# Five gate tiles of a hybrid decoder step move from behind the recurrence into the turns of its heads

## The chip, the core and the metric

The kernel runs on one core of a Trainium2 chip, as one launch. The metric is the time of one execution in microseconds (us) of the device. Five engines take part: TensorE (PE in the profile), VectorE (DVE), ScalarE (ACT), GpSimd (POOL) and SyncE (SP), which only issues transfers. Each engine works through its own list of instructions in order and waits at semaphores for the others.

## The reference

One layer of a decoder with two groups of mixers, for 256 tokens of a prompt and 8 sequences of 8 new tokens, so 320 token columns in all. What matters here is the input projection and the second group, a gated linear recurrence over eight heads of 128 channels:

```python
h = rms_norm(x, norm1[l])
z = h @ w_in[l]
u, q, f, i, g = jnp.split(z, [...])            # pooling input, then 8 heads each of q, f, i, g
...
forget = lb + (1.0 - lb) * jax.nn.sigmoid(f)
logf, k_in, q_f = jnp.log(forget), 1.0 - forget, jax.nn.silu(q)
o, S_new = hgrn2_recurrence(heads(q_f), heads(k_in), heads(i), heads(logf), S_prev[l])
o = o * lax.rsqrt(jnp.mean(o * o, axis=-1, keepdims=True) + EPS)   # per head
o = o * hg_norm[l]
o = o.reshape(B, T, HG_WIDTH) * jax.nn.silu(g)                     # the output gate
mix = jnp.concatenate([pool_out, o], axis=-1) @ w_o[l]
x = x + mix
```

A SwiGLU feed-forward of width 5632 and a last norm follow. All is in fp32.

## The kernel before

**Tiles.** Every projection is cut into tiles of 128 output channels, called units here, with running numbers: 8 of the pooling group, then `H0` on three for each head (forget, query, value), then from `G0` on eight gate tiles (one for each head), then 16 of the output projection from `O0` on, then the feed-forward. A unit of `w_in` is 16 tiles of 128x128 weights; for each, TensorE makes three matmuls over the 320 token columns (weights high x activations high, high x low, low x high), so 48 matmuls. `unit` runs eight weight tiles, then what is given as `between[0]`, the other eight, then `between[1]`. Units alternate between two PSUM banks `zb[0]` and `zb[1]`.

**Splits.** The weights of a unit are loaded by SP into `raw` (two buffers, 1 MB each; a load waits until the unit two before it is split), and split into a high part by ScalarE (`split_hi`, L682) and a low part by VectorE (`split_lo`, L1013), two pieces each. A high piece waits until TensorE has used the same piece of the unit two before. The low piece waits for the high piece. VectorE reads a finished unit from PSUM (`scaled`, L1022), and a unit waits until the unit two before it has been read.

**The recurrence.** It runs in turns of three units. While TensorE works on the forget, query and value units of head h, the recurrence of head r = h - 1 is woven in, in this order (L572): half of the forget unit, `rec_scores(r)`, the other half, `rec_state(r)`, half of the query unit, `rec_out(r)`, the other half, `rec_stat(r)` (the mean of squares over the channels of a head, L391), the value unit, `rec_bcast(r)` (L397 to L400: the reciprocal root of each token is spread over all partitions; it waits for `odiag`, the diagonal matrices that `rec_rms` makes on VectorE).

```python
unit(n, par_, a_rhs, between=(at(rec_scores) if r is not None else extra[0], at(rec_state)))
unit(n + 1, 1 - par_, a_rhs, between=(at(rec_out), at(rec_stat)))
unit(n + 2, par_, a_rhs, between=(extra[1], at(rec_bcast) if not last else None))
```

In the same turn VectorE does, in order (L1289): split of unit n+1, placing of the scores (`rec_scores`), `rec_sample_lo`, reading of the forget unit into `zf`, `rec_state`, split of n+2, `rec_sample_state`, `products(h)` (the products of forget factors, L1177), reading of the query unit into `zq`, split of n+3, `rec_rms(r)` (a reciprocal, four small Newton steps, two diagonals: L1255, L1082 to L1092), `queries(h)` (L1184, L1190), reading of the value unit, `rec_norm(r)`, `rec_lo(r)`. ScalarE does: split of n+1, `rec_tokens`, `forget(h)` (sigmoid of `zf`, then the factors `t`, on which `products` waits), split of n+2, `rec_squares(r)`, the transfers of states, `sigmoid_q(h)`, split of n+3, `rec_std(r)` (the square root, L825; it ends in `ostd`, on which `rec_rms` waits), `rec_hi(r)`. GpSimd makes keys (L1490, L1498) and queries (L1504) of head h, and the decayed sample states.

Heads 0 and 7 are handled at the ends; heads 1 to 6 as r lie in a loop of three rounds with two turns each.

**The gate tiles.** The last turn has the recurrence of head 7 and the units of gates 0, 1 and 2; the units of gates 3 to 7 stand alone behind it, with the `rec_bcast` of head 7 after five weight tiles of gate 3 (L588). A gate costs: VectorE reads the unit into `zf`; ScalarE takes its sigmoid (L839); GpSimd multiplies (L1537); VectorE sums the two parts of the head's mixed output into `go` (L1281), multiplies by the gate (L1285); ScalarE and VectorE split the result again (L843, L1025). The output projection takes the mixed output of head h as its weight tile 8 + h.

Of the kernel before, what the change touches and what calls it, by code (L numbers as in the profile page):

```python
# [26 lines left out]
P = 128  # L27
D = 2048
KD = D // P
# [7 lines left out]
PW = 1024  # L37
# [4 lines left out]
HEADS = 8  # L42
# [21 lines left out]
G0 = H0 + 3 * HEADS  # L64
O0 = G0 + HEADS
# [27 lines left out]
def hybrid_kernel(nc, x_prompt, x_sample, cache_pool, state_hgrn, lb_param, norm1, w_in, w_pool, pool_scale,  # L93
# [12 lines left out]
    with ctx:  # L106
# [73 lines left out]
        go = vv  # L180
# [111 lines left out]
        def _(sp):  # L292
# [27 lines left out]
            with sp.Fori(0, HEADS // 2) as i:  # L320
                for k in range(2):
                    for j, part in enumerate((2, 1, 3)):
                        load(H0 + 6 * i + 3 * k + j, (3 * k + j) % 2, win_v, (0, KD),
                             part * PW + (2 * i + k) * P)
            with sp.Fori(0, HEADS // 2) as i:
                for k in range(2):
                    load(G0 + 2 * i + k, k, win_v, (0, KD), 4 * PW + (2 * i + k) * P)
# [22 lines left out]
        def _(pe):  # L350
# [141 lines left out]
            def rec_scores(r):  # L492
# [32 lines left out]
                pe.wait_ge(unit_read, H0 + 3 * r + 3)  # L525
# [46 lines left out]
            def window(n, par_, r, extra=(None, None), last=False):  # L572

                def at(f):
                    return (lambda: f(r)) if r is not None else None
                unit(n, par_, a_rhs, between=(at(rec_scores) if r is not None else extra[0], at(rec_state)))
                unit(n + 1, 1 - par_, a_rhs, between=(at(rec_out), at(rec_stat)))
                unit(n + 2, par_, a_rhs, between=(extra[1], at(rec_bcast) if not last else None))

            window(H0, 0, None, (lambda: pool_states(NG - 1), lambda: pool_product(NG - 1)))  # L580
            window(H0 + 3, 1, 0)
            with pe.Fori(0, (HEADS - 2) // 2) as i:
                window(H0 + 6 + 6 * i, 0, 2 * i + 1)
                window(H0 + 9 + 6 * i, 1, 2 * i + 2)

            window(G0, 0, HEADS - 1, last=True)

            def last_bcast(k):  # L588
                if k == 4:
                    rec_bcast(HEADS - 1)  # L590
            unit(G0 + 3, 1, a_rhs, after_tile=last_bcast)
            with pe.Fori(0, (HEADS - 4) // 2) as i:
                for k in range(2):
                    unit(G0 + 4 + 2 * i + k, k, a_rhs)
# [77 lines left out]
        def _(act):  # L672
# [96 lines left out]
            def forget(h):  # L769

                act.wait_ge(unit_read, H0 + 3 * h + 1)
                after(act, q_ready, h)
                act.activation(sgm[:, :], zf[:, :], ACT.Sigmoid).then_inc(zf_sig, 1)
# [6 lines left out]
            def sigmoid_q(h):  # L780
                act.wait_ge(unit_read, H0 + 3 * h + 2)
# [50 lines left out]
            def gate(h):  # L832

                gate_sigmoid(h)
                gate_split(h)

            def gate_sigmoid(h):
                act.wait_ge(unit_read, G0 + h + 1)
                act.activation(sgm[:, :], zf[:, :], ACT.Sigmoid).then_inc(g_sig, 1)  # L839
# [5 lines left out]
            def window(n, par_, h, r):  # L845
# [3 lines left out]
                forget(h) if h is not None else gate(0)  # L849
                split_hi(n + 2, par_)  # L850
                rec_squares(r)
                if h is not None:
                    load_s0(r + 1)
                rec_stores(r)
                sigmoid_q(h) if h is not None else gate(1)
                split_hi(n + 3, 1 - par_)
                rec_std(r)
                if h is None:
                    gate(2)
                else:  # L860
                    rec_hi(r)


# [7 lines left out]
            forget(0)  # L871
            split_hi(H0 + 2, 0)
            sigmoid_q(0)
# [5 lines left out]
            with act.Fori(0, (HEADS - 2) // 2) as i:  # L879
                window(H0 + 6 + 6 * i, 0, 2 * i + 2, 2 * i + 1)  # L880
                window(H0 + 9 + 6 * i, 1, 2 * i + 3, 2 * i + 2)

            act.wait_ge(out_done, 32)
            window(G0, 0, None, HEADS - 1)
            split_hi(G0 + 4, 0)
            gate_sigmoid(3)
            rec_hi(HEADS - 1)
            gate_split(3)
            with act.Fori(0, (HEADS - 4) // 2) as i:
                for k in range(2):  # L890
                    split_hi(G0 + 5 + 2 * i + k, 1 - k)
                    gate(4 + 2 * i + k)
# [103 lines left out]
        def _(dve):  # L996
# [274 lines left out]
            def gate(n, par_, h):  # L1271

                gate_read(n, par_)
                gate_apply(h)

# [3 lines left out]
            def gate_apply(h):  # L1279
# [3 lines left out]
                dve.wait_ge(osum, h + 1)  # L1283
                dve.wait_ge(g_act, h + 1)
# [3 lines left out]

            def window(n, par_, h, r):  # L1289

                split_lo(n + 1, 1 - par_)
                if r is not None:
                    rec_scores(r)
                    rec_sample_lo(r)
                scaled(n, par_, zf[:, :]).then_inc(unit_read, 1)
                if r is not None:
                    rec_state(r)
                if h is None:
                    gate_apply(0)
                split_lo(n + 2, par_)  # L1300
                if r is not None:
                    rec_sample_state(r)
                else:
                    pool_means(NG - 1)
                    dve.wait_ge(t_ones, 1)
                if h is not None:
                    products(h)
                    scaled(n + 1, 1 - par_, zq[:, :]).then_inc(unit_read, 1)
                else:
                    gate(n + 1, 1 - par_, 1)  # L1310
                split_lo(n + 3, 1 - par_)
                if r is not None:
                    rec_rms(r)
                if h is not None:
                    queries(h)
                if h is not None:
                    if r is None:
                        pool_lo(NG - 1)
                        dve.wait_ge(sc_zero, 1)
                    done(n + 2)  # L1320
                    out, src = thrice(v_rep, zb[par_])
                    dve.tensor_tensor(out, src, thrice(v_rep, rbc)[1], MUL).then_inc(v_thrice, 1)
                    scaled(n + 2, par_, vv[:, :]).then_inc(unit_read, 1)
                else:
                    gate(n + 2, par_, 2)
                if h is not None and r is not None:
                    rec_norm(r)
                    rec_lo(r)

            window(H0, 0, 0, None)  # L1330
            window(H0 + 3, 1, 1, 0)
            with dve.Fori(0, (HEADS - 2) // 2) as i:
                window(H0 + 6 + 6 * i, 0, 2 * i + 2, 2 * i + 1)
                window(H0 + 9 + 6 * i, 1, 2 * i + 3, 2 * i + 2)

            window(G0, 0, None, HEADS - 1)
            split_lo(G0 + 4, 0)
            gate_read(G0 + 3, 1)
            rec_norm(HEADS - 1)
            rec_lo(HEADS - 1)  # L1340
            gate_apply(3)
            with dve.Fori(0, (HEADS - 4) // 2) as i:
# [248 lines left out]
```

## Time and profile before

| | |
|---|---|
| median of 3 runs | 1489.78 us (1488.51 to 1493.13) |
| the profiled execution | 1493.66 us |
| span of its instructions | 1491.4 us |
| mean granted TensorE clock | 0.992 of full speed |
| busy: PE, DVE, ACT, POOL | 1460.7, 804.9, 550.8, 188.2 us |
| stages | pooling units to 99 us; heads to 395 us, gates alone to 428 us, output projection to 541 us, feed-forward to 1477 us |

In the rows further down, times are microseconds from the start of the span unless marked ns. A row of the timeline is: start, time, engine, line of the kernel and operation, output <- inputs, shape, xcount, and in brackets the idle time before it with what ended it. Durations of matmuls overlap, since they are pipelined: the step from one start to the next is what TensorE really spends.

### The profile page before, as it was taken

To read this page: it belongs to the slowest core of one execution; us is meant where nothing else is said; L and a number is where in the kernel's file an instruction comes from. 1 tells how busy PE (TensorE), PEld (TensorE's weight loads), DVE (VectorE), ACT (ScalarE), POOL (GpSimd) and SP (SyncE) were. 2 spreads that over 40 slices of the span, in tenths; PEclk is the share of its full clock that TensorE was granted. 3 is DMA by queue.
4 is the path that set the end of the run, shared out by engine and by line. 5 is a ranking of instruction groups with operands and counts; after the bars stand their busy time and mean duration, and the time that the engine had idled before them with its cause. 6 is when DMAs were issued, how large, how long until landed. Compare 5 with 4: busy or idle time off the path is not lost.

```text
span 1491.4 us, 27027 instructions
## 1 busy us (share of the span) xinstructions
PE 1460.7 (98%) x9928; PEld 1440.6 (97%) x9928; DVE 804.9 (54%) x1200; ACT 550.8 (37%) x823; POOL 188.2 (13%) x202
## 2 busy tenths in 40 slices
PE   7999999999999999999999999999999999999996
PEld 5999999999999999999999999999999999999996
DVE  4657788787665554444444444444444444444443
ACT  6443433344443343333333333333333333333443
POOL 0244434333112210000000000000000000000131
PEclk9999999999999999999999999999999999999998
DMA  8445444434455555554565555565554556555453
GB/s 222 136 127 143 128 127 131 114 114 138 114 162 143 153 144 153 141 160 125 146 187 142 141 142 141 144 164 153 157 141 134 151 146 164 154 151 141 119 148 114
DMA packets 409519, 214.52 MB, mean 144 GB/s; under 512 B 4093, under 2 KB 407757, under 8 KB 409420
## 3 DMA queue, kind: packets, MB, share of 16 engines
q1 hardware_dynamic: 391207, 203.52, 49.8%
q10 hardware_dynamic: 18277, 10.52, 2.5%
q8 instruction: 23, 0.38, 0.1%
q14 instruction: 12, 0.10, 0.0%
HBM read 206.14 MB, written 7.89 MB: 144 GB/s over the span
## 4 chain that ended last, share of the span: by engine, by line
PE 85%; DVE 9%; issue 3%; ACT 2%; DMA 1%; DVEq 0%; ACTq 0%; SPq 0%
PE bank L366 27%; PE bank L367 27%; PE bank L368 27%; DVE qr L1190 2%; DVE w_lo L1013 2%; DVE t L1177 1%; ACT w_hi L682 1%; DVE sc L1205 1%; PE bank L507 1%; DMA xt<-in_x_sample 1%; DVE sn L1249 0%; PE bank L462 0%; PE bank L410 0%; PE bank L538 0%; PE bank L412 0%
## 5 line engine op out<-in xcount | busy, mean ns | idle before, releaser
L366 PE MATMUL bank<-a_hi,w_hi 128*128 128x320 f32 x2048 | 642.4, 314 | 0.0
L367 PE MATMUL bank<-a_lo,w_hi 128*128 128x320 f32 x2048 | 636.1, 311 | 0.0
L368 PE MATMUL bank<-a_hi,w_lo 128*128 128x320 f32 x2048 | 635.9, 311 | 0.0
L1013 DVE TENSOR_TENSOR w_lo<-w_raw,w_hi 128x1024 fp32r<-128x1024 f32 (+1 forms) x416 | 467.3, 1164 | 150.3 <-ACT w_hi L682 149.5
L682 ACT ACTIVATE w_hi<-w_raw 128x1024 fp32r<-128x1024 f32 (+1 forms) x416 | 387.3, 967 | 158.6 <-PE bank L368 148.5
L366 PEld LDWEIGHTS bank<-a_hi,w_hi 128*128 128x128 f32 x2048 | 387.6, 189 | 2.4
L367 PEld LDWEIGHTS bank<-a_lo,w_hi 128*128 128x128 f32 x2048 | 387.7, 189 | 0.8
L368 PEld LDWEIGHTS bank<-a_hi,w_lo 128*128 128x128 f32 x2048 | 387.3, 189 | 0.0
L366 PE MATMUL bank<-h_hi,w_hi 128*128 128x320 f32 x704 | 217.7, 309 | 0.0
L367 PE MATMUL bank<-h_lo,w_hi 128*128 128x320 f32 x704 | 216.6, 308 | 0.0
L368 PE MATMUL bank<-h_hi,w_lo 128*128 128x320 f32 x704 | 216.5, 308 | 0.0
L367 PEld LDWEIGHTS bank<-h_lo,w_hi 128*128 128x128 f32 x704 | 132.0, 187 | 0.0
L366 PEld LDWEIGHTS bank<-h_hi,w_hi 128*128 128x128 f32 x704 | 132.0, 187 | 0.0
L368 PEld LDWEIGHTS bank<-h_hi,w_lo 128*128 128x128 f32 x704 | 131.9, 187 | 0.0
L1562 POOL TENSOR_TENSOR sq<-x 128x320 f32<-128x320 f32 x15 | 10.8, 720 | 903.1 <-DVE x L1399 903.1
L909 ACT ACTIVATE h_hi<-hid 128x320 f32 (+1 forms) x44 | 20.7, 472 | 238.3 <-DVE hid L1367 238.3
L1401 DVE TENSOR_TENSOR x_res<-x_res,bank 128x320 f32 (+1 forms) x48 | 23.4, 488 | 120.7 <-PE bank L368 120.7
L1022 DVE TENSOR_TENSOR zu<-bank,rms_bc 128x320 f32<-128x320 f32 x44 | 21.6, 491 | 120.3 <-PE bank L368 120.3
L905 ACT ACTIVATE sg<-zg 128x320 f32<-128x320 f32 x44 | 20.8, 472 | 175.5 <-DVE zg L1022 175.5
L1022 DVE TENSOR_TENSOR zg<-bank,rms_bc 128x320 f32<-128x320 f32 x44 | 21.6, 491 | 86.4 <-PE bank L368 86.3
L1498 POOL TENSOR_TENSOR kx<-kx,t 128x256 f32<-128x256 f32 (+1 forms) x56 | 48.7, 870 | 30.8 <-DVE t L1177 27.5
L366 PE MATMUL bank<-mp_hi,w_hi 128*128 128x320 f32 x128 | 39.4, 308 | 0.0
(218 smaller groups left out, 1186.5 us busy)
## 6 DMA issues: line engine op xcount, KB each, us to landing
w_raw<-in_w_gate SPq DMA_DIRECT2D x44, 1024.0 KB, 5.6
w_raw<-in_w_up SPq DMA_DIRECT2D x44, 1024.0 KB, 5.6
w_raw<-in_w_down SPq DMA_DIRECT2D x64, 704.0 KB, 4.8
w_raw<-in_w_in SPq DMA_DIRECT2D x39, 1024.0 KB, 5.8
w_raw<-in_w_o SPq DMA_DIRECT2D x16, 1024.0 KB, 6.1
s<-in_state_hgrn ACTq DMA_DIRECT2D x8, 512.0 KB, 4.3
out<-sn ACTq DMA_DIRECT2D x8, 512.0 KB, 7.2
xt<-in_x_prompt SPq DMA_DIRECT2D x3, 512.0 KB, 9.4
```

The lines of the kernel that those rows point to most:

```text
L366: pe.matmul(out, whi[:, par_, cols], r_hi, start=(k == 0), stop=False)
L367: pe.matmul(out, whi[:, par_, cols], r_lo, start=False, stop=False)
L368: last = pe.matmul(out, wlo[:, par_, cols], r_hi, start=False, stop=(k == last_k))
L507: last = pe.matmul(bk[:, at + c * 64:at + c * 64 + 64].rearrange("p (m j) -> p m j", j=2 ** l), kx[l][:, c * CH:(c + 1) * CH], right_half( ...
L682: act.activation(whi[:, par_, k0 * P:k1 * P], raw[:, par_, k0 * P:k1 * P], ACT.Copy)\
L905: act.activation(sg[:, :], zg[:, :], ACT.Silu).then_inc(gate_act, 1)
L909: act.activation(h_hi[:, j, :], hid[:, :], ACT.Copy).then_inc(hid_hi, 1)
L1013: dve.tensor_tensor(wlo[:, par_, cols], raw[:, par_, cols], whi[:, par_, cols].bitcast(F32), SUB)\
L1022: return dve.tensor_tensor(out, zb[par_][:, 0:N], rbc[:, :], MUL)
L1190: dve.tensor_tensor(blocks_of(qr[l + 1], l, n), blocks_of(qr[l], l, n), times(l, n, 0), MUL)\
L1401: dve.tensor_tensor(x1[:, j, :], x1[:, j, :], zb[par_][:, 0:N], ADD).then_inc(unit_read, 1)
L1498: pool.tensor_tensor(blocks_of(kx[l + 1], l, n), blocks_of(kx[l], l, n), times(l, n, 2), MUL)\
```

## The change

Five of the eight gate tiles get a place inside the loop of turns. Each of the turns with r = 1 to 5 now has four units: first the gate unit of head g = r - 1, then forget, query and value of head r + 1. The recurrence pieces of head r keep their places by position (scores and state in and after the first unit, outputs and mean in and after the second, the broadcast after the third), so they now lie around gate, forget and query; the value unit comes last with nothing in it. The turn of r = 6 has three units as before. Behind it stand the gate units of heads 5, 6 and 7 with the recurrence of head 7, whose broadcast comes after nine weight tiles of the last of them; and the gate of head 7 multiplies `on` directly, without splitting it first. `go` shares the buffer of `on` and no longer that of `vv`. The diff, cut to its core:

```diff
-G0 = H0 + 3 * HEADS
-O0 = G0 + HEADS
+EARLY = 5
+W2 = H0 + 6
+W7 = W2 + 4 * EARLY
+G0 = W7 + 3
+O0 = G0 + HEADS - EARLY
...
-        go = vv
+        go = on
...
+            with sp.Fori(0, EARLY) as i:
+                load(W2 + 4 * i, 0, win_v, (0, KD), 4 * PW + i * P)
+                for j, part in enumerate((2, 1, 3)):
+                    load(W2 + 4 * i + 1 + j, 1 - j % 2, win_v, (0, KD), part * PW + (i + 2) * P)
...
-                pe.wait_ge(unit_read, H0 + 3 * r + 3)
+                pe.wait_ge(unit_read, n)
...
+            def window(n, par_, r, count):
+
+                unit(n, par_, a_rhs, between=(lambda: rec_scores(r, n), lambda: rec_state(r)))
+                unit(n + 1, 1 - par_, a_rhs, between=(lambda: rec_out(r), lambda: rec_stat(r)))
+                unit(n + 2, par_, a_rhs, between=(None, lambda: rec_bcast(r)))
+                if count == 4:
+                    unit(n + 3, 1 - par_, a_rhs)
...
+            window(H0 + 3, 1, 0, 3)
+            with pe.Fori(0, EARLY) as i:
+                window(W2 + 4 * i, 0, i + 1, 4)
+            window(W7, 0, HEADS - 2, 3)
...
             def last_bcast(k):
-                if k == 4:
+                if k == HEADS:
                     rec_bcast(HEADS - 1)
...
+            unit(G0, 1, a_rhs, between=(lambda: rec_scores(HEADS - 1, G0), lambda: rec_state(HEADS - 1)))
+            unit(G0 + 1, 0, a_rhs, between=(lambda: rec_out(HEADS - 1), lambda: rec_stat(HEADS - 1)))
+            unit(G0 + 2, 1, a_rhs, after_tile=last_bcast)
...
+            def gate_window(n, g, h, r):
+
+                split_hi(n + 1, 1)
+                rec_tokens(r)
+                gate_sigmoid(g, n, r)
+                split_hi(n + 2, 0)
+                gate_split(g)
+                rec_squares(r)
+                load_s0(h)
+                rec_stores(r)
+                forget(h, n + 1, g + 1)
+                split_hi(n + 3, 1)
+                rec_std(r)
+                sigmoid_q(h, n + 2)
+                split_hi(n + 4, 0)
+                rec_hi(r)
...
+            split_hi(G0 + 1, 0)
+            rec_tokens(HEADS - 1)
+            gate_sigmoid(EARLY, G0, HEADS - 1)
+            split_hi(G0 + 2, 1)
+            gate_split(EARLY)
+            rec_squares(HEADS - 1)
+            rec_stores(HEADS - 1)
+            gate_sigmoid(EARLY + 1, G0 + 1, HEADS - 1)
+            split_hi(O0, 0)
+            gate_split(EARLY + 1)
+            rec_std(HEADS - 1)
+            gate_sigmoid(EARLY + 2, G0 + 2, HEADS - 1)
+            gate_split(EARLY + 2)
...
+            def gate_window(n, g, h, r):
+
+                split_lo(n + 1, 1)
+                rec_scores(r)
+                rec_sample_lo(r)
+                gate_read(n, 0)
+                rec_state(r)
+                split_lo(n + 2, 0)
+                gate_apply(g)
+                rec_sample_state(r)
+                scaled(n + 1, 1, zf[:, :]).then_inc(unit_read, 1)
+                split_lo(n + 3, 1)
+                products(h)
+                rec_rms(r)
+                scaled(n + 2, 0, zq[:, :]).then_inc(unit_read, 1)
+                split_lo(n + 4, 0)
+                queries(h)
+                rec_norm(r)
+                rec_lo(r)
+                values(n + 3, 1)
...
+            gate_read(G0, 1)
+            rec_state(HEADS - 1)
+            split_lo(G0 + 2, 1)
+            gate_apply(EARLY)
+            rec_sample_state(HEADS - 1)
+            gate_read(G0 + 1, 0)
+            split_lo(O0, 0)
+            gate_apply(EARLY + 1)
+            rec_rms(HEADS - 1)
+            gate_read(G0 + 2, 1)
             rec_norm(HEADS - 1)
-            rec_lo(HEADS - 1)
...
+            dve.wait_ge(on_ready, HEADS)
+            gate_product(HEADS - 1)
...
+            with pool.Fori(0, EARLY) as i:
+                rec_sample(i + 1)
+                gate(i)
+                keys(i + 2)
+                query(i + 2)
+                key_copies(i + 2)
```

The first `gate_window` is ScalarE's, the second VectorE's; `values` reads the value unit as before.

## Rows read from the trace of the kernel before

**Rows 1.** The page: busy time of each engine, its share and instructions.

```profile
PE 1460.7 (98%) x9928; PEld 1440.6 (97%) x9928; DVE 804.9 (54%) x1200; ACT 550.8 (37%) x823; POOL 188.2 (13%) x202
```

**Rows 2.** Windows of the span: one turn, and the output projection alone.

```profile
198.00:232.00 34.00, 32.65 (x238) 31.49 (x237) 27.11 (x53) 13.59 (x25) 13.46 (x13) 1.00 0.45 127
...
428.40:541.00 112.60, 112.60 (x770) 112.60 (x769) 64.16 (x66) 39.85 (x49) 25.16 (x32) 1.00 0.55 149
```

**Rows 3.** Waits of TensorE: for whom, us in total, times, longest.

```profile
PE bank L397 <- DVE dg L1092: 4.4, 5, 1.0
PE bank L507 <- issue: 3.1, 6, 0.5
```

**Rows 4.** Timeline of TensorE, heads 0, 2, 6 and 7 as r.

```profile
124.50 1.55 PE L507 MATMUL bank<-qr,kx 128*128 128x64 f32 x12 [1.32 <-DVE mp_lo L1148]
...
146.99 0.70 PE L391 MATMUL bank<-mean_cols,dg 128*128 128x1 f32 x6
...
154.77 0.48 PE L397 MATMUL bank<-dg,ones_mat 128*128 128x128 f32 x2
...
209.43 0.74 PE L560 MATMUL bank<-vm,k 96*128 96x512 f32 x2
...
213.53 0.70 PE L391 MATMUL bank<-mean_cols,dg 128*128 128x1 f32 x6
...
222.30 0.49 PE L397 MATMUL bank<-dg,ones_mat 128*128 128x128 f32 x2 [0.83 <-DVE dg L1092]
...
345.07 1.21 PE L560 MATMUL bank<-vm,k 96*128 96x512 f32 x2
...
350.71 0.70 PE L391 MATMUL bank<-mean_cols,dg 128*128 128x1 f32 x6
...
384.52 0.71 PE L391 MATMUL bank<-mean_cols,dg 128*128 128x1 f32 x6
```

**Rows 5.** Timeline of VectorE in the turn of head 2.

```profile
205.21 0.49 DVE L1022 TENSOR_TENSOR zf<-bank,rms_bc 128x320 f32<-128x320 f32 x1
...
208.04 3.04 DVE L1013 TENSOR_TENSOR w_lo<-w_raw,w_hi 128x1024 fp32r<-128x1024 f32 x2 [1.76 <-ACT w_hi L682]
...
212.20 3.31 DVE L1177 TENSOR_TENSOR t<-t 128x160 f32<-128x160 f32 x7
215.44 0.48 DVE L1022 TENSOR_TENSOR zq<-bank,rms_bc 128x320 f32<-128x320 f32 x1
217.40 3.35 DVE L1013 TENSOR_TENSOR w_lo<-w_raw,w_hi 128x1024 fp32r<-128x1024 f32 x2 [1.49 <-ACT w_hi L682]
220.67 0.16 DVE L1255 RECIPROCAL stat<-stat 128x3 f32<-128x3 f32 x1
...
222.68 5.16 DVE L1190 TENSOR_TENSOR qr<-qr,t 128x320 f32<-128x320 f32 x7
```

**Rows 6.** Timeline of ScalarE, head 2 as r, and the split of head 7.

```profile
206.97 1.98 ACT L682 ACTIVATE w_hi<-w_raw 128x1024 fp32r<-128x1024 f32 x2
...
218.61 1.28 ACT L825 ACT_TABLE_LOAD   x1
219.91 0.26 ACT L825 ACTIVATE stat<-bank,eps_col 128x2 f32<-128x2 f32 x1
...
387.68 1.99 ACT L682 ACTIVATE w_hi<-w_raw 128x1024 fp32r<-128x1024 f32 x2
```

**Rows 7.** Timeline of VectorE in the last turn, head 7 as r.

```profile
384.72 0.49 DVE L1022 TENSOR_TENSOR zf<-bank,rms_bc 128x320 f32<-128x320 f32 x1 [1.69 <-PE bank L368]
...
388.76 2.36 DVE L1013 TENSOR_TENSOR w_lo<-w_raw,w_hi 128x1024 fp32r<-128x1024 f32 x2 [0.46 <-ACT w_hi L682]
391.70 0.18 DVE L1255 RECIPROCAL stat<-stat 128x3 f32<-128x3 f32 x1 [0.58 <-ACT stat L826]
```

**Rows 8.** Windows around two falls of the granted clock (column PEclk).

```profile
126.00:130.00 4.00, 4.00 (x26) 3.82 (x25) 3.19 (x8) 0.00 (x0) 0.00 (x0) 0.58 0.25 68
...
344.00:348.00 4.00, 4.00 (x19) 3.62 (x19) 4.00 (x5) 1.37 (x3) 1.65 (x1) 0.64 0.26 60
```

More of the change, by code:

```diff
@@ L767, in _, with forget @@
                     pool_hi(g - 1)
-            def forget(h):
-                act.wait_ge(unit_read, H0 + 3 * h + 1)
+            def forget(h, n, gates=0):
+                act.wait_ge(unit_read, n + 1)
                 after(act, q_ready, h)
+                after(act, g_act, gates)
                 act.activation(sgm[:, :], zf[:, :], ACT.Sigmoid).then_inc(zf_sig, 1)
@@ L830, in rec_hi, with gate_sigmoid @@
                 act.activation(bh_hi[:, r, :], on[:, :], ACT.Copy).then_inc(mh_hi_s, 1)
[L832 to L838, printed above, removed]
+            def gate_sigmoid(h, n, head):
+                act.wait_ge(unit_read, n + 1)
+                act.wait_ge(q_ready, head + 1)
                 act.activation(sgm[:, :], zf[:, :], ACT.Sigmoid).then_inc(g_sig, 1)
@@ L878, in _ @@
             window(H0 + 3, 1, 1, 0)
-            with act.Fori(0, (HEADS - 2) // 2) as i:
-                window(H0 + 6 + 6 * i, 0, 2 * i + 2, 2 * i + 1)
-                window(H0 + 9 + 6 * i, 1, 2 * i + 3, 2 * i + 2)
+            with act.Fori(0, EARLY) as i:
+                gate_window(W2 + 4 * i, i, i + 2, i + 1)
+            window(W7, 0, HEADS - 1, HEADS - 2)
             act.wait_ge(out_done, 32)
[L884 to L892, printed above, removed]
+            split_hi(G0 + 1, 0)
[11 more added lines that the diff above has]
+            gate_split(EARLY + 2)
             def h2_part(j):
@@ L1340, in _ @@
[L1340 to L1345 removed]
+                rec_sample_state(r)
+                products(h)
+                scaled(n + 1, 1 - par_, zq[:, :]).then_inc(unit_read, 1)
+                split_lo(n + 3, 1 - par_)
+                rec_rms(r)
+                queries(h)
@@ new lines, in window @@
+                values(n + 2, par_)
+                rec_norm(r)
+                rec_lo(r)
+            def gate_window(n, g, h, r):
+                split_lo(n + 1, 1)
+                rec_scores(r)
+                rec_sample_lo(r)
+                gate_read(n, 0)
+                rec_state(r)
+                split_lo(n + 2, 0)
+                gate_apply(g)
+                rec_sample_state(r)
+                scaled(n + 1, 1, zf[:, :]).then_inc(unit_read, 1)
+                split_lo(n + 3, 1)
+                products(h)
+                rec_rms(r)
+                scaled(n + 2, 0, zq[:, :]).then_inc(unit_read, 1)
+                split_lo(n + 4, 0)
+                queries(h)
+                rec_norm(r)
+                rec_lo(r)
+                values(n + 3, 1)
@@ new lines, in _ @@
+            split_lo(H0 + 1, 1)
+            scaled(H0, 0, zf[:, :]).then_inc(unit_read, 1)
+            split_lo(H0 + 2, 0)
+            pool_means(NG - 1)
+            dve.wait_ge(t_ones, 1)
+            products(0)
+            scaled(H0 + 1, 1, zq[:, :]).then_inc(unit_read, 1)
+            split_lo(H0 + 3, 1)
+            queries(0)
+            pool_lo(NG - 1)
+            dve.wait_ge(sc_zero, 1)
+            values(H0 + 2, 0)
+            window(H0 + 3, 1, 1, 0)
+            with dve.Fori(0, EARLY) as i:
+                gate_window(W2 + 4 * i, i, i + 2, i + 1)
```

131 lines of the change are left out of this document (36 added, 95 removed).

## The prediction, made before the changed kernel had run

> **What bounds the kernel now.** I read the page first. TensorE is busy for 98% of the span, no other engine for more than 54% [rows 1]. The reader should see that nothing can be gained by giving other engines less to do, only by closing holes in TensorE's work. The number of units stays at 208, so the change is worth the holes that it closes less those that it opens. The windows show where holes can be: none in the output projection (112.60 busy of 112.60, 770 matmuls, 0.147 us each), but 1.35 us in a turn of 34 us [rows 2]. The waits name them: five broadcasts of a head (L397) waited for the diagonals of VectorE, 4.4 us together, and six starts of the scores (L507) waited 3.1 us for "issue", 0.5 us each, in the loop [rows 3]. The timeline gives the hole its true size. Without a wait, the step from the start of the mean (L391) to the broadcast (L397) is 154.77 - 146.99 = 7.78 us (0.63 for the mean, 48 matmuls for the rest). For head 2 it is 222.30 - 213.53 = 8.77, so 0.99 are lost where the row says 0.83 [rows 4], since the modelled end of a matmul reaches 0.16 further. All five: 4.4 + 5 x 0.16 = 5.2 us.
>
> **Why the broadcast is late now.** On VectorE [rows 5] the products run before the query unit is read (215.44), then comes the split of the next unit, then the reciprocal (220.67), and 222.30 - 220.67 = 1.63 us later the broadcast starts. Between reading a unit and the reciprocal there lies only one split: 220.67 - 215.44 = 5.2 us.
>
> **The change, part by part.** The deadline of the broadcast stays where it was: behind the third unit of the turn, 7.78 us after the second is finished. What changes is what VectorE must do between those two points. The second unit is now the forget unit, and its consumers come after its reading: ScalarE's sigmoid and factors, ScalarE's high split of n+3 queued behind them, VectorE's low split, then `products`, then `rec_rms`. With rows:
>
> - From the finished unit (the start of L391) to its reading: 384.72 - 384.52 = 0.20 us [rows 4, 7].
> - From that reading to the end of the low split: ScalarE starts the high split at 206.97, 1.76 after the reading at 205.21; VectorE's low split runs from 208.04 to 211.08. Together 5.87 us [rows 5, 6]. That is the same sequence (forget read, sigmoid, factors, split) beside the same key operations of GpSimd, so I take it whole. Its lower bound is the low split of 2.36 instead of 3.04 [rows 7], when GpSimd stays away: 5.2.
> - `products`: 3.31 until the last piece ends, 3.24 to the next start [rows 5]; I take 3.25.
> - `rec_rms` to the broadcast: 1.63.
>
> Sum: 0.20 + 5.87 + 3.25 + 1.63 = 10.95 us against 7.78, a hole of **3.2 us** in each gate turn (2.5 at the lower bound). ScalarE's `rec_std` doesn't set it: the high split ends 208.95 - 205.21 = 3.7 us after the reading [rows 5, 6] and `rec_std` about 2 us later (the tail, below, has its rows), before `products` even starts. Nor does the first unit's gate: its sum, product and splits fit while TensorE works on the second unit; `rec_sample_state` then has until the unit ends. Five turns: 5 x 3.2 = **16 us**.
>
> **What is late next?** Behind the broadcast's diagonals VectorE reads the query unit, splits n+4 and runs `queries`. From reading to the end of that split it is 217.40 + 3.35 - 215.44 = 5.3 us, and the queries are 0.5 + 5.16 more [rows 5], 11.0 in all. TensorE wants them after the broadcast (1.0), the value unit (48 x 0.147 = 7.05) and half a gate unit (3.5), at 11.6. So 0.6 us are left, and I cost it at nothing; without the hole in front of the broadcast that cover would be gone too. VectorE's sum over a gate turn (27.1 of the old turn [rows 2], 2.0 for the gate, 3.0 for a fourth split) is 32 us in a turn of 40, so the engine isn't short of time, only its order is late.
>
> **The turn of head 6** has its old order, but begins with VectorE 2 us ahead (the value unit is read last in the turn before, and its transposes wait for nothing). The products then wait for the sample state, and the hole is some 0.3 us. It also leaves the loop, as one of the six waits of 0.5 us at the scores does [rows 3]: -0.5.
>
> **The tail.** The broadcast of head 7 came after two whole units less 11 tiles; now it comes 9 weight tiles after the mean: 0.63 + 27 x 0.147 = 4.6 us after the finished unit. Before it VectorE must read the unit (0.2 to 0.7), ScalarE take the sigmoid and begin the high split at about 1.2, the low split ends 388.76 + 2.36 - 387.68 = 3.44 later [rows 6, 7] at 4.6, the sum and product of gate 6 take 1.0 (5.6), ScalarE's `gate_split` 0.5 (6.1), and only then, in its queue, comes `rec_std`: from the end of the split at 389.67 to the reciprocal at 391.70 it is 2.03 (8.1) [rows 6, 7], and `rec_rms` 1.63 more (9.8). A hole of 9.8 - 4.6 = **5.2 us**. What follows isn't late: the last gate is wanted by weight tile 15 of `O0`, 6.6 us into it, and is ready about 4 us in. The rounding away of one split of head 7 saves only ScalarE and VectorE 1.5 us that lie beside this.
>
> In this tail a table load of 1.28 us is on the path. The profile has the next activation 0.02 us behind the load (218.61 + 1.28 = 219.89, then 219.91) [rows 6]. The Trainium skill ("ScalarE: Activation LUTs", What ACT_TABLE_LOAD costs) adds a drain of about 1.38 us to each load; by the page the tail's hole would be 6.6 instead of 5.2, and the trace speaks for the smaller. In the gate turns the number of loads stays at two.
>
> **Moved transfers.** SP issues the same loads of 1 MB in the new order, each as before behind the split of the unit two before; ScalarE issues the same state transfers, behind `gate_split`, some 2 us later than before and 15 us ahead of their use. Nothing.
>
> **The clock.** The granted clock fell to its lower level (1.2 of 2.4 GHz) where TensorE had idled 1.32 us and then did the small matmuls of scores [rows 4, 8], and after the small matmuls of `rec_out` of head 6. The latter cost 350.71 - 345.07 = 5.64 against 213.53 - 209.43 = 4.10, so 1.54 us [rows 4]; head 7 had one like it. It didn't fall after the holes of about 1 us. Holes of 3.2 and 5.2 us are longer than any in the middle of this kernel, so between 0 and 7 new falls of 1.5 us are possible. I take 4: **+6 us**, as a hole of 3.2 is nearer to the case that fell than to those that didn't.
>
> **Sum.** -5.2 - 0.5 + 16 + 0.3 + 5.2 + 6 = +21.8. The profiled execution took 1493.66 (span 1491.4), so it would take 1515.5; it stands 3.9 above the median of the runs, which gives 1489.8 + 21.8 = **1511.5 us**, 1.5% slower.
>
> **Rivals.**
> 1. *The forecast:* the broadcast waits in each gate turn and in the tail. 0.80; about 0.55 of it with several falls of the clock (1507 to 1517), 0.25 with none or one (1503 to 1507: 1489.8 + 15.8 = 1505.6).
> 2. *Faster:* the broadcast is in time. It decides at the order on VectorE: if the low split of n+3 and the products were through 7.78 - 1.63 = 6.1 us after the second unit, the hole would be nil. For it: each turn has 7 us more of TensorE's work and only 5 of VectorE's. Against: the split alone ends at 6.07. If the tail's broadcast were in time too, 1489.8 - 5.2 - 0.5 + 0.3 = 1484.4. 0.07.
> 3. *No change:* the gate turns are covered, but the tail's hole remains: 1484.4 + 5.2 = 1489.6. 0.04.
> 4. *Worse:* the holes also make the queries late, by more than the 0.6 us of slack, or every hole brings a fall or two: 1489.8 + 15.8 + 7 x 1.54 = 1516.4, and 1 to 2 us more in each turn gives up to 1525. For it: [rows 8] show the clock low after short idling. The Trainium skill ("TensorE: Matmul & The Clock Gate", HAM oscillation) also has each burst behind an idle gap start at half clock. 0.09.
>
> **Range.** Low: five holes of 2.5 (-3.4), no fall (-6) and the lowest run (-1.3) give 1500.8. High: seven falls and a late query or two, 1519. I give 1500 to 1519. A measurement of this kernel can tell about 0.3%, 4.5 us: slower by more 0.89, within 0.04, faster 0.07.
>
> **What would show it.** L397 waits for `dg` in five gate turns with some 3 us each, once in the tail with 5, and for little in the turn of head 6; L391 to L397 steps 10.95. VectorE between the forget reading and the reciprocal has split and products back to back. The clock falls just behind some of these. It would be wrong if ScalarE's high split of n+3 stood ahead of the sigmoid's wait, if the products overlapped the split, or if the holes are there and the time isn't, because something earlier in the turn had cost as much.

## The result, and the profile after

The changed kernel took 1521.8 us (median of 4 runs, 1516.1 to 1528.7) against 1491.45 us of the kernel before (4 runs): a ratio of 1.0207, 95% interval 1.0161 to 1.0254, so 30 us slower. The forecast was 1511.5 and its range ended at 1519. The profiled execution took 1522.0 (span 1520.2), 28.8 us more than the span of before. The page after: busy times, TensorE's busy share in 40 slices (tenths), and the shares of the chain of work that ended last:

```profile
span 1520.2 us, 26900 instructions
PE 1470.2 (97%) x9928; PEld 1450.6 (95%) x9928; DVE 805.6 (53%) x1198; ACT 562.0 (37%) x831; POOL 187.5 (12%) x202
PE   7999998888989999999999999999999999999996
...
PE 90%; DVE 5%; issue 2%; ACT 1%; DMA 1%; DVEq 0%; ACTq 0%; SPq 0%
```

The same 9928 matmuls, with slices of TensorE below 90% in the heads' stage. The waits of TensorE answer to [rows 3]:

```profile
PE bank L403 <- DVE dg L1111: 25.3, 6, 4.8
PE bank L416 <- DMA xt<-in_x_sample: 7.7, 1, 7.7
...
PE bank L513 <- issue: 0.5, 1, 0.5
```

The broadcast (now L403) waited six times, 25.3 us, and the scores (now L513) once where they had waited six times for "issue". TensorE's timeline, turns of heads 1 and 3 and the tail, answers to [rows 4]:

```profile
180.94 0.75 PE L397 MATMUL bank<-mean_cols,dg 128*128 128x1 f32 x6
...
193.59 0.80 PE L403 MATMUL bank<-dg,ones_mat 128*128 128x128 f32 x2 [4.67 <-DVE dg L1111]
...
272.36 0.70 PE L397 MATMUL bank<-mean_cols,dg 128*128 128x1 f32 x6
...
284.27 0.49 PE L403 MATMUL bank<-dg,ones_mat 128*128 128x128 f32 x2 [3.97 <-DVE dg L1111]
...
297.44 0.27 PE L502 MATMUL bank<-cst,kx 128*128 128x128 f32 x1
...
441.56 0.71 PE L397 MATMUL bank<-mean_cols,dg 128*128 128x1 f32 x6
...
451.19 0.80 PE L403 MATMUL bank<-dg,ones_mat 128*128 128x128 f32 x2 [4.78 <-DVE dg L1111]
```

From the mean (L397) to the broadcast it is 284.27 - 272.36 = 11.91 us against 7.78 without a wait: a hole of 4.1 us in the turns of heads 2 to 5, and 12.65 - 7.78 = 4.9 in that of head 1. In the tail the broadcast stands 21 matmuls of 0.147 us earlier, so 4.7 without a wait, and 9.63 - 4.7 = 4.9. VectorE in the turn of head 3, and GpSimd beside it, answer to [rows 5]:

```profile
272.56 0.49 DVE L1041 TENSOR_TENSOR zf<-bank,rms_bc 128x320 f32<-128x320 f32 x1 [2.23 <-PE bank L374]
275.40 3.05 DVE L1032 TENSOR_TENSOR w_lo<-w_raw,w_hi 128x1024 fp32r<-128x1024 f32 x2 [2.35 <-ACT w_hi L688]
278.37 3.29 DVE L1196 TENSOR_TENSOR t<-t 128x160 f32<-128x160 f32 x7
281.58 0.16 DVE L1274 RECIPROCAL stat<-stat 128x3 f32<-128x3 f32 x1
281.78 0.16 DVE L1101 TENSOR_TENSOR stat<-stat 128x3 f32<-128x3 f32 x1
281.98 0.48 DVE L1102 TENSOR_TENSOR stat<-stat 128x3 f32<-128x3 f32 x1
282.49 0.17 DVE L1103 TENSOR_SCALAR stat<-stat 128x3 f32<-128x3 f32 x1
282.69 0.54 DVE L1104 TENSOR_TENSOR stat<-stat 128x3 f32<-128x3 f32 x1
283.27 0.42 DVE L1108 TENSOR_TENSOR dg<-cst,stat 128x256 f32<-128x256 f32 x1
283.61 0.60 DVE L1111 TENSOR_SCALAR dg<-cst,stat 64x64 f32<-64x64 f32 x1
```

```profile
281.80 0.64 POOL L1537 TENSOR_TENSOR kx<-kx,t 128x256 f32<-128x256 f32 x1 [0.16 <-DVE t L1196]
282.60 0.62 POOL L1537 TENSOR_TENSOR kx<-kx,t 128x256 f32<-128x256 f32 x1 [0.16 <-POOL kx L1537]
283.38 0.79 POOL L1537 TENSOR_TENSOR kx<-kx,t 128x256 f32<-128x256 f32 x1 [0.16 <-POOL kx L1537]
```

The order is as forecast: the forget unit is read 0.20 behind its end, the split ends 5.9 behind the reading, the products follow, then the small steps. But from the reciprocal to the broadcast it is 284.27 - 281.58 = 2.69 us, not 1.63: three of the small operations take 0.48, 0.54 and 0.60, where they took 0.16, 0.16 and 0.24 before, while GpSimd multiplies keys. Each of the three begins while a key product is under way and ends when that product ends, to within 0.04 us (282.46 and 282.44, 283.23 and 283.22, 284.21 and 284.17); of the four that kept their time, the first began 0.07 before the end of a product and the others in the pauses of 0.16 us between two. The windows behind the broadcasts, with the granted clock (third number from the end), answer to [rows 8]:

```profile
284.20:288.20 4.00, 3.93 (x16) 3.69 (x17) 2.52 (x4) 2.36 (x3) 3.01 (x3) 0.59 0.00 0
288.20:292.20 4.00, 4.00 (x29) 4.00 (x28) 3.90 (x5) 0.00 (x0) 1.17 (x1) 0.99 0.06 15
373.70:377.70 4.00, 3.96 (x14) 3.62 (x15) 2.52 (x3) 2.36 (x3) 2.83 (x3) 0.50 0.00 0
377.70:381.70 4.00, 4.00 (x21) 4.00 (x20) 3.90 (x5) 0.00 (x0) 2.30 (x1) 0.65 0.57 163
```

All six holes were followed by the lower clock. From the broadcast to the next scores' transposes (L502) TensorE needs 11.56 us at full clock (as in all gate turns of run 1, below); it took 14.3, 13.2, 13.2, 13.2 and 14.7, so 10.73 too many, and 2.03 more in the tail. Of the two falls behind `rec_out` that the kernel before had in the turns of heads 6 and 7 (3.1 us together) one was left, of 1.5 us.

**Where the difference lies**, in the two profiled executions:

| us | forecast | measured |
|---|---|---|
| holes at five broadcasts closed | -5.2 | -5.2 |
| waits at the scores closed | -0.5 | -3.7 |
| five gate turns | +16 | 4.9 + 4 x 4.13 = +21.4 |
| turn of head 6 | +0.3 | 0 |
| tail | +5.2 | +4.9 |
| falls of the clock | +6 | 12.8 + 1.5 - 3.1 = +11.2 |
| first transfer of x later | | +1.1 |
| sum | +21.8 | +29.7 (the spans differ by 28.8) |

The waits at the scores: the step from the transposes (L494) to L513 is 0.22 us after, in every turn but the first; before it was 0.90, six times (and 0.48 once). What the scores waited for can be read in the kernel before: the queries of VectorE ended at 222.68 + 5.16 = 227.84 [rows 5], and the scores started 0.20 us behind them.

```profile
228.04 1.52 PE L507 MATMUL bank<-qr,kx 128*128 128x64 f32 x12 [0.52 <-issue]
```

So it is in all six: they start 0.20 to 0.22 us behind the last of the queries. In the changed kernel the queries of the turn of head 3 end at 294.27 and the scores start at 297.87, with nothing to wait for.

### The profile page after: what moved, and what is told of

Its sections match the earlier page's. It is cut to its first block, busy times and chain, and to the rows that moved or that the text cites. A ratio compares the mean times of both kernels' runs of the same rounds, so it can differ in the third digit from the quotient of the medians.

```text
span 1520.2 us, 26900 instructions
## 1 busy us (share of the span) xinstructions
PE 1470.2 (97%) x9928; PEld 1450.6 (95%) x9928; DVE 805.6 (53%) x1198; ACT 562.0 (37%) x831; POOL 187.5 (12%) x202
## 4 chain that ended last, share of the span: by engine, by line
PE 90%; DVE 5%; issue 2%; ACT 1%; DMA 1%; DVEq 0%; ACTq 0%; SPq 0%
PE bank L372 28%; PE bank L373 28%; PE bank L374 28%; PE bank L513 2%; DVE t L1196 1%; DVE w_lo L1032 1%; PE bank L544 1%; ACT w_hi L688 1%; DMA xt<-in_x_sample 1%; DVE qr L1209 1%; PE bank L468 0%; PE bank L416 0%; PE bank L566 0%; PE bank L418 0%; PE bank L403 0%
```

## Experiments

The table compares each kernel with the kernel before on the same chip; line numbers are those of the changed kernel, shifted by a few where lines were added.

| run | median us | before us | ratio, 95% interval |
|---|---|---|---|
| changed kernel | 1521.8 | 1491.45 | 1.0207 (1.0161 to 1.0254) |
| rms first | 1518.1 | 1490.9 | 1.0194 (1.0162 to 1.0225) |
| keys held | 1507.6 | 1490.9 | 1.0113 (1.0077 to 1.0149) |
| holes filled | 1511.3 | 1490.9 | 1.0147 (1.0116 to 1.0179) |
| tail moved | 1517.8 | 1490.9 | 1.0180 (1.0116 to 1.0244) |
| gate tile last | 1494.3 | 1492.8 | 1.0012 (0.9995 to 1.0029) |
| filled, tail moved | 1507.1 | 1492.8 | 1.0092 (1.0069 to 1.0115) |
| filled, last gate split first | 1512.65 | 1492.8 | 1.0136 (1.0113 to 1.0160) |
| reordered | 1489.5 | 1492.8 | 0.9989 (0.9968 to 1.0009) |
| reordered, all keys held | 1530.3 | 1491.2 | 1.0276 (1.0252 to 1.0299) |
| reordered, keys 1 to 6 held | 1521.8 | 1491.2 | 1.0222 (1.0197 to 1.0247) |
| reordered, keys 3 to 6 held | 1492.1 | 1492.4 | 0.9997 (0.9979 to 1.0014) |

**1. Rms first.** In the gate turns VectorE runs `rec_rms` ahead of `products`.

```diff
                 split_lo(n + 3, 1)
-                products(h)
                 rec_rms(r)
+                products(h)
```

> The changed kernel, but in the five gate turns VectorE runs rec_rms ahead of products. Theory (the broadcast is late because split and products of the forget unit stand before rec_rms on VectorE): the split ends 6.1 us behind the forget unit, rec_rms takes 1.6 us there since GpSimd has nothing to do then, so the broadcast starts at 7.75 where TensorE wants it at 7.78: the holes of 4.1 us are gone, and their falls of the clock with them (some 21 + 10 us). What is late next by the same sums: the queries, ready about 21.1 us behind the forget unit (in the changed kernel they end 10.1 us behind the reading of the query unit) against 19.6, so a new hole of some 1.5 to 2.2 us in front of the scores of heads 2 to 6; 1522 - 31 + 9 = 1500 if the clock stays, up to 1512 if it falls there. Rival (the four-unit turn is bound by work somewhere else, and the broadcast only shows it): the hole moves in full and the time stays at 1518 to 1525.

The broadcast is in time in every gate turn. TensorE's timeline in the turn of head 2:

```profile
223.54 0.71 PE L397 MATMUL bank<-mean_cols,dg 128*128 128x1 f32 x6
...
231.32 0.38 PE L403 MATMUL bank<-dg,ones_mat 128*128 128x128 f32 x2
...
245.49 1.52 PE L513 MATMUL bank<-qr,kx 128*128 128x64 f32 x12 [2.00 <-issue]
```

231.32 - 223.54 = 7.78: no hole. It stands at the scores now, 2.0 us, five times; the label "issue" hides that the scores wait for the queries, which ended at 240.32 + 4.96 = 245.28:

```profile
240.32 4.96 DVE L1209 TENSOR_TENSOR qr<-qr,t 128x320 f32<-128x320 f32 x7
```

The clock fell behind these too, all five times, and for longer (0.61 and 0.54 in the next two stretches): it cost 4.9 us once and 3.3 us four times, where the falls behind the broadcasts had cost 1.6 to 3.1. Small matmuls follow here, at the broadcast dense ones; that this is why it lasts longer isn't shown.

```profile
247.00:251.00 4.00, 4.00 (x27) 3.81 (x25) 2.88 (x4) 3.20 (x5) 0.00 (x0) 0.61 0.00 0
251.00:255.00 4.00, 4.00 (x19) 3.98 (x19) 2.68 (x11) 2.28 (x5) 0.00 (x0) 0.54 0.62 184
```

So the cause of the broadcast's wait is shown to be the order on VectorE. But the gain was under 4 us: the time lay 6 us above the upper end that my theory gave, and inside the range of its rival. The rival's mechanism, that the hole moves in full, isn't what happened (2.0 us of 4.1 moved); I had counted a fall at the scores as dear as one at the broadcast.

**2. Keys held.** GpSimd waits for the diagonals before the key products of level 1 and on, which make the keys of level 2 and on.

```diff
                     if l:
                         pool.wait_ge(prod_ready, LP * h + l)
+                    if l == 1 and hold:
+                        pool.wait_ge(odiag, h)
```

> The changed kernel, but in the gate turns GpSimd makes the keys of level 2 and on only after the diagonals of the head before are done, so that it is idle during rec_rms. Theory (rec_rms takes 2.7 us instead of 1.6 because GpSimd's key products run beside it): rec_rms falls to 1.6 us, the holes from 4.1 to about 3.1, the time by 4 to 6 us to 1517, fewer if a fall of the clock stays or moves. Rival (rec_rms is long for its own reasons, as waits in a longer loop body): rec_rms stays at 2.7 us, time 1520 to 1524.

VectorE in the turn of head 3, and the broadcast and scores behind it:

```profile
272.64 1.86 DVE L1196 TENSOR_TENSOR t<-t 128x160 f32<-128x160 f32 x7
274.42 0.17 DVE L1274 RECIPROCAL stat<-stat 128x3 f32<-128x3 f32 x1
...
275.77 0.24 DVE L1111 TENSOR_SCALAR dg<-cst,stat 64x64 f32<-64x64 f32 x1
```

```profile
276.06 0.49 PE L403 MATMUL bank<-dg,ones_mat 128*128 128x128 f32 x2 [1.71 <-DVE dg L1111]
...
289.61 1.52 PE L513 MATMUL bank<-qr,kx 128*128 128x64 f32 x12 [1.28 <-issue]
```

The step from the reciprocal to the broadcast falls from 2.69 to 1.64, as expected. What I hadn't expected is that `products` fall from 3.29 to 1.86: they too had been slowed, and the 3.31 us of the kernel before [rows 5] look the same. Together that is 2.5 us; the hole fell by 2.3, from 4.1 to 1.9 (9.64 - 7.78), as the split ended 0.2 later. In the turn of head 1 it fell from 4.9 to 2.7. Only two of these five holes, both of 1.9 us, were followed by a fall. In three turns the scores now waited, 1.3 us, since VectorE's queries had to wait for GpSimd's query product. The time fell by 14 us, three times what I had expected, as the holes shrank more than expected and fewer falls followed.

**3. Holes filled.** Idle matmuls of the projection's size in front of the broadcasts; nothing reads what they write.

```diff
+            def fill(r, count):
+                pe.wait_ge(s2_ready, r + 1)
+                for _ in range(count):
+                    pe.matmul(SC[:, 0:N], a_hi[:, 0, 0:P], a_hi[:, 1, :], start=True, stop=True)
...
+                def third():
+                    if count == 4:
+                        fill(r, 27)
+                    rec_bcast(r)
```

> The changed kernel with idle matmuls in the holes: 27 matmuls of the size of the projection's (4.0 us) in front of each broadcast of the gate turns and 30 (4.4 us) in front of that of head 7, into a free bank; nothing reads them. Theory (the clock falls because TensorE idles in those holes): the holes are filled, the broadcasts start when they did, the clock no longer falls behind them: six falls and 12.5 us less, 1509 to 1511. Rival (the falls come from the small matmuls of the recurrence or from where they lie, as two did before the change): the clock falls as before, time 1520 to 1524, or more by what the filling overshoots.

The stretches around the broadcast of the turn of head 3 (281.57) have the full clock:

```profile
279.70:283.70 4.00, 3.97 (x26) 3.52 (x25) 2.41 (x7) 1.75 (x3) 2.66 (x5) 1.00 0.26 65
283.70:287.70 4.00, 4.00 (x30) 4.00 (x29) 4.00 (x3) 0.62 (x1) 2.99 (x2) 1.00 0.00 0
```

Not one broadcast was followed by a fall, and the time was 1511.3, in the expected 1509 to 1511 but for 0.3: 10.5 us less for doing useless work (by the ratios to the kernel before, 1.0207 and 1.0147, it is 9 us). That TensorE's idling brings these falls is shown. The Trainium skill ("TensorE: Matmul & The Clock Gate", HAM oscillation) says the same of gaps between bursts; this run agrees.

**4. Tail moved,** and **5. filled, tail moved.** The broadcast of head 7 after five weight tiles of the first output unit; once in the changed kernel, once with the gate turns filled.

```diff
             def last_bcast(k):
-                if k == HEADS:
+                if k == 4:
                     rec_bcast(HEADS - 1)
...
-            unit(G0 + 2, 1, a_rhs, after_tile=last_bcast)
+            unit(G0 + 2, 1, a_rhs)
...
-            unit(O0, 0, m_rhs, tile_wait=m_tile)
+            unit(O0, 0, m_rhs, tile_wait=m_tile, after_tile=last_bcast)
```

> The changed kernel, but the broadcast of head 7 comes after five weight tiles of the first output unit instead of nine of the last gate unit. Theory: the hole of 4.9 us and the fall behind it (2.0 us) go, and the last gate is still ready some 2 us before weight tile 15 wants it: 1522 - 7 = 1515. Rival (the last gate becomes late instead): part of it comes back as a wait of the output projection, 1517 to 1521.

> As the run that fills the holes with idle matmuls, but in the tail nothing is filled and the broadcast of head 7 comes in the first output unit. It measures the tail's hole without the clock's scatter: theory 4.9 us less than with the filled hole, 1506 to 1507. Rival (the tail only moves its wait to the last gate): 1509 to 1511.

The first took 1517.8 with runs from 1506.7 to 1525.6: too wide to tell. In its profile the tail had no wait, but there were four falls behind `rec_out`, where the changed kernel had one. The second, where no broadcast is followed by a fall, tells it: 1507.1 against 1511.3, 4.2 us of the tail's 4.9, and no wait for the last gate. The two were timed on different chips; by their ratios to the kernel before, 1.0092 and 1.0147, it would be 0.0055 x 1491 = 8 us, so the move is worth 4 to 8 us.

**6. Filled, last gate split first.** The output of head 7 is split and summed before its gate, as before the change, with the holes filled.

```diff
-            dve.wait_ge(on_ready, HEADS)
-            gate_product(HEADS - 1)
+            rec_lo(HEADS - 1)
+            dve.wait_ge(mh_lo_s, HEADS)
+            gate_apply(HEADS - 1)
```

> As the run that fills the holes with idle matmuls, but the output of head 7 is split and summed again before its gate, as in the kernel before. Theory: the direct gate takes some 1.6 us off VectorE's and ScalarE's list, of which the first half of the second output unit's split was late by next to nothing; so 0 to 1 us more, 1511 to 1512. Rival (the direct gate is worth its whole time): 1513.

1512.65 against 1511.3. In its profile the second output unit waits 0.65 us for its split. By the medians the direct gate is worth about 1 us; but the two were timed on different chips, and by the ratios (1.0136 and 1.0147) the difference has the other sign. So its worth in time isn't shown, only the wait of 0.65 us.

**7. Gate tile last.** The turn is forget, query, value, gate; the old order of VectorE, then the gate; the split of the next unit ahead of the queries; tail moved. GpSimd's and ScalarE's lists are changed to match. The core of it, on VectorE:

```diff
+                scaled(n, 0, zf[:, :]).then_inc(unit_read, 1)
                 rec_state(r)
                 split_lo(n + 2, 0)
-                gate_apply(g)
                 rec_sample_state(r)
-                scaled(n + 1, 1, zf[:, :]).then_inc(unit_read, 1)
-                split_lo(n + 3, 1)
                 products(h)
+                scaled(n + 1, 1, zq[:, :]).then_inc(unit_read, 1)
+                split_lo(n + 3, 1)
                 rec_rms(r)
-                scaled(n + 2, 0, zq[:, :]).then_inc(unit_read, 1)
                 split_lo(n + 4, 0)
                 queries(h)
+                values(n + 2, 0)
                 rec_norm(r)
                 rec_lo(r)
-                values(n + 3, 1)
+                gate_read(n + 3, 1)
+                dve.wait_ge(mh_lo_s, r + 1)
+                gate_apply(g)
```

> The changed kernel with the gate tile as the last unit of its turn instead of the first (forget, query, value, gate), the old order of VectorE and ScalarE before it, the split of the next unit moved ahead of the queries, the gate applied at the turn's end, and the broadcast of head 7 in the first output unit. Theory (what costs time is which unit stands between the forget unit and the broadcast, not that there is a gate tile in the turn): the query unit is read before the broadcast is wanted, VectorE enters each turn earlier, holes of 0 to 0.5 us at the broadcasts (1.0 in the kernel before), no wait at the scores, no new falls of the clock: 1481 to 1487. Rival (a fourth unit's work on VectorE and ScalarE makes a turn late wherever it stands): holes of 2 us or more remain in each turn, 1495 or more.

1494.3 us, 27 less than the changed kernel. The moved tail is 4 to 8 of these (run 5); the rest goes with the gate's place and the orders that came with it, which this run doesn't separate. But it is no faster than the kernel before, and my forecast of it missed: four of five gate turns still had holes of 1.7 to 2.3 us at the broadcast (316.15 - 306.70 = 9.45 against 7.78), one of them with a fall of the clock behind it, and TensorE waited 2.0 us in all for the reading of value units. VectorE is late in these turns: in the one shown it reads the query unit (second row) 2.6 us behind its end. In the turn of head 3, where the clock had just fallen behind `rec_out` and given VectorE 1.5 us, it reads it 0.2 behind, and there is no hole. I take it that the gate and the queries of the turn before, still on VectorE's list, make it late; no run tests that alone:

```profile
306.70 0.71 PE L397 MATMUL bank<-mean_cols,dg 128*128 128x1 f32 x6
...
309.30 0.48 DVE L1041 TENSOR_TENSOR zq<-bank,rms_bc 128x320 f32<-128x320 f32 x1
...
316.15 0.49 PE L403 MATMUL bank<-dg,ones_mat 128*128 128x128 f32 x2 [1.52 <-DVE dg L1111]
```

**8. Reordered.** The changed kernel with `products` and `rec_rms` ahead of the split of n+3, and the tail moved.

```diff
-                split_lo(n + 3, 1)
                 products(h)
                 rec_rms(r)
+                split_lo(n + 3, 1)
```

> The changed kernel, but VectorE runs products and rec_rms of the gate turns ahead of the split of n+3, and the broadcast of head 7 comes in the first output unit. Theory: products start as soon as the factors are there (2.0 us behind the forget unit), the diagonals are done at 8.3 to 8.7, so holes of 0.5 to 1 us at the broadcast; the first piece of the split is 0 to 0.5 late; the queries are next late, by about 1 us, as in the run with rec_rms first but less: 1491 to 1499 by how often the clock falls. Rival (VectorE's whole list behind the forget unit is too long, whatever its order): holes of 3 us or more in each turn, 1508 or more.

1489.5 us, a little below what was expected: 32 us less than the changed kernel by moving one line on VectorE and one broadcast. The hole left is 1.3 us (1.9 in the first gate turn), and no fall followed one:

```profile
267.20 0.49 PE L403 MATMUL bank<-dg,ones_mat 128*128 128x128 f32 x2 [1.13 <-DVE dg L1111]
```

**9 to 11. Reordered, keys held.** As in 2, on this kernel, from level 0, 1 or 3 on.

```diff
+                    if l == 0 and hold:      # or 1, or 3
+                        pool.wait_ge(odiag, h)
                     pool.wait_ge(kx_ready, (LP + 1) * h + l + 1)
```

> The reordered kernel (products and rec_rms ahead of the split of n+3, broadcast of head 7 in the first output unit), and GpSimd holds back all key products of a gate turn until the diagonals are done. Theory (the rest of the hole, 1.2 to 1.3 us in each gate turn, is VectorE slowed by GpSimd's key products beside it): products take 1.9 instead of 4.1 us, rec_rms 1.6 instead of 2.6 but not before ScalarE's root at 6.0 us, so the diagonals are ready at 7.7 and the hole is gone; 5 to 6 us less, 1483 to 1487. Rival (what GpSimd does later comes in the way of the split and the queries instead): a wait of 0.5 us or more before the next unit or before the scores, 1488 or more.

> The same, but only the key products from level 1 on are held back; the first two run beside the products of VectorE as long as these wait for ScalarE. Theory: products some 0.8 us longer than with all held back, still before the root is there, so the same holes and a shorter list for GpSimd afterwards: the same time to 1 us less. Rival: products reach past the root, 1 to 3 us more.

> The reordered kernel again, with only the last four key products (levels 3 to 6) held back until the diagonals are done. In the reordered kernel those four ran beside rec_rms (2.6 us instead of 1.6) and ended at the time at which the query's sigmoid was ready. Theory: rec_rms takes 1.6, the hole of 1.2 us falls to 0 to 0.4 us, and the query product, which waits for its sigmoid anyway, is late by no more than 0.5 us, less than the slack of the queries: 1483 to 1486. Rival (any delay on GpSimd moves the wait to the scores, as when all key products were held back): waits of 1 us or more at the scores and new falls of the clock, 1492 or more.

All three close the hole at the broadcast, but for 0.6 to 0.8 us in the first gate turn and, in the third, 0.2 to 0.3 in the others; and all three open one at the scores: 4.3, 3.0 and 1.2 us, in that order.

```profile
300.43 1.94 PE L513 MATMUL bank<-qr,kx 128*128 128x64 f32 x8 [4.33 <-issue]
```

VectorE of the first of them shows what I had left out, the query product of GpSimd, which is queued behind the keys and on which the queries wait (waits of VectorE: line, us in total, times, longest):

```profile
DVE qr L1203 <- POOL qq L1545: 18.6, 5, 3.7
```

In the first the rival won, at 1530.3. The second, 1521.8, fits neither expectation: it should have been at most 1 us faster than the first, or slower, and is 8 us faster, since GpSimd's list behind the diagonals is shorter and the scores wait 1.3 us less in each turn. With four products held it is 1492.1, as the rival has it: the 1.2 us at the broadcast moved to the scores; but none of these waits was followed by a fall. No version was shown to beat the kernel before; the reordered one comes nearest, and its interval holds 1.

## Why the prediction was wrong

**Right:** the sign and the place. The broadcast waited in all five gate turns and in the tail, for little or nothing in the turn of head 6, and for the reason given: the split and the products of the forget unit stand before `rec_rms` on VectorE (shown by runs 1 and 8). The split and the products were sized rightly: 5.89 and 3.21 us for 5.87 and 3.25. The tail's 5.2 us was 4.9 in the profile, 4 to 8 in time (run 5). Its table load had no added drain: the reciprocal followed at 8.0 us, as reckoned, so the smaller price was right.

**Wrong, first:** the term "`rec_rms` to the broadcast: 1.63". It came from a turn in which GpSimd had nothing to do at that moment. I had asked of the split whether GpSimd would stay away (the lower bound) but not, of the step behind the products, whether it would come in: in the new order the keys of the same head follow each product at once, and reach into `rec_rms`. It measured 2.69, and 1.64 again when GpSimd was held back (run 2), so 3.2 us was 4.1; the first turn was 0.7 more, since VectorE came late to the forget unit there (0.86 behind its end instead of 0.20). Together 5.4 us.

**Wrong, second:** the step "between 0 and 7 new falls of 1.5 us are possible. I take 4". There were six, and three cost 2.0 to 3.1 us each, as the clock stayed low for longer. Run 3 puts the six at 9 to 10.5 us in time. The forecast's own upper rival (seven falls at 1.54) had the number nearly right and the size too small. Either error alone would have left the time inside the range (1511.5 + 5.4 or + 5.2); both together took it out. The argument for 4 was also weak: it went by the length of the hole alone, and length alone doesn't decide, as the last section shows.

**Wrong, third, the other way:** the wait at the scores. I read "issue" in [rows 3] as a cost of waits in a loop, and took 0.5 us as gone. It was the wait for the queries: in the trace of the kernel before they end 0.20 to 0.22 us ahead of the scores each time, in run 1 the wait grew to 2.0 when they were later, and it went in all but one turn of the changed kernel, where the holes gave VectorE time. That is 3.7 us gained instead of 0.5. By luck this error hid 3 us of the other two.

**The slack.** "0.6 us are left" behind the broadcast measured 1.8: in the turn of head 3 the queries end 10.0 us behind the broadcast, and at full clock the scores would have started 11.56 + 0.44 = 12.0 behind it, 0.2 of which they need. Costing it at nothing was right. Closing the hole of 4.1 us should then make the queries late by 4.1 - 1.8 = 2.3, and in run 1 it was 2.0. In other words VectorE's list from the forget unit to the queries was 2 us longer than TensorE's time, and the hole at the broadcast hid it. About 1 us of the sum stays open.

## What to carry to other kernels

When work is put between a producer and a consumer that has a fixed place in another engine's order, don't add busy times; walk the in-order list from the last input to the deadline, and then walk on to the next deadline: in runs 1 and 9 to 11, closing one hole opened the next, of 1.2 to 4.3 us. Take each duration from a stretch in which the same neighbours run; and price a hole of TensorE with the fall of the clock that can follow it (1.6 to 4.9 us here), not by its length alone.

## What the runs showed of the hardware

- GpSimd beside VectorE: seven products of 3.29 us took 1.86 with GpSimd held back, and from the reciprocal to the broadcast it was 1.64 us instead of 2.69. In each gate turn of the changed kernel a VectorE instruction that began while a GpSimd product was under way ended when the product ended, to within 0.05 us: two 128x3 `tensor_tensor` of 0.16 us took 0.48 and 0.54, a 64x64 `tensor_scalar` of 0.24 took 0.60. Those that began in the pause of 0.16 us between two products kept their time, also a 128x256 `tensor_tensor` (0.42). The Trainium skill ("GPSIMD Engine Reference", Specifications) names SBUF interfaces shared with VectorE, in contention with its instructions that have two SBUF inputs or run in a 2-port mode; the two `tensor_tensor` agree. The `tensor_scalar` has a single tensor input, and whether it runs in such a mode no run shows.
- The lower clock behind holes of 4 to 5 us cost 1.6 to 3.1 us each, and all six of the changed kernel were followed by it. So were the five holes of 2.0 us before the scores in run 1, at 3.3 to 4.9 us each. Of the holes of 1.3 to 1.9 us before dense work in the reordered kernel none was; of the five of 1.8 to 2.7 us in run 2 two were, of the four of 1.7 to 2.3 in run 7 one. Useless matmuls in the hole kept the clock up and saved 9 to 10.5 us.
- The length of a hole alone doesn't decide. The one of 1.3 us before the first scores was followed by the lower clock (0.50) in ten of the thirteen profiles and not in those of runs 1, 9 and 10 (1.00 throughout); the five of 1.2 us before the same small matmuls in run 11 were not. What else decides isn't shown.
